# Head norms of a dilated attention computed inside the input projection instead of in the attention's own block

## The chip, the cores and the metric

The kernel runs on one core of a Trainium2 chip, in one launch. The metric is the device time of that core in microseconds (us). All weights (626 MB) are streamed from HBM, each once; everything is float32, and the large products are made of three products of split operands.

## What is computed

Two transformer blocks follow each other on 256 tokens of width 2048. The first block has an adaptive norm, an input projection `w_in` into u, q, k and v (1024 columns each), a state-space mixer on u, a dilated attention on q, k, v, an output projection and a gated FFN. The second block has two FFNs and another mixer. What the change touches is the attention of the first block:

```python
q = _rms(q.reshape(B, S, N_HEADS, HEAD_DIM), q_norm_w) * (HEAD_DIM ** -0.5)
k = _rms(k.reshape(B, S, N_HEADS, HEAD_DIM), k_norm_w)
slopes = exp2(-arange(1, 9))            # 8 heads of 128
bias = -slopes[:, None, None, None] * (dilation * dist)
scores = where(valid, q @ k.T + bias, MASK_VALUE)
```

`_rms` divides every head's vector of a token by the root of its mean square. So there are 16 head sums for each token (8 of q, 8 of k), 16 factors 1/root, and each score is q.k times a factor of the query and a factor of the key, plus a bias that depends on the distance and the head.

## The kernel before, in words

Activations lie transposed: features on the 128 partitions, tokens along the free axis (272 columns, of which 256 are the sequence). TensorE (PE), ScalarE (ACT), VectorE (DVE), GpSimd (POOL) and the DMA issuer SyncE (SP) have programs of their own, which meet in semaphores. The program is written in blocks; at the end of a block all engines meet.

**The input projection** (`products(pe, "w_in", ...)`, lines 551 to 553) is 32 chunks, counted by `m` from 0 to 31. A chunk of weights is a DMA of 1 MB into `raw`; ACT rounds it into `w_hi` (`split_hi`, L413), DVE subtracts into `w_lo` (`split_lo`, L418), and PE does 48 matmuls of 256 columns on it. Both `w_hi` and `w_lo` have two buffers, so ACT may split chunk m once chunk m-2 is multiplied. Between its splits DVE also accumulates rows of the adaptive weights for gate 1 (`condition`, L432, four products a chunk), and PE sums those over the partitions with `gather` (L437, four matmuls with one moving column of ones, for each of eight groups).

Beside each chunk a piece of the state-space mixer runs (`ssm_pe`, `ssm_act`, `ssm_dve`). It has 8 blocks `i`, and a block has three slots, `m = 5 + 3i + slot` on PE: slot 0 is 8 transposes (L1226), slot 1 the inputs to the states and the powers (L1236, L1246, L1247), slot 2 the outputs (L1261, L1263) and, before the change, the gathers of gate 1 (`GATE1_AT`). ACT and DVE do their part one chunk later.

**The attention's block** comes next. `heads_act`, `heads_pe` and `heads_dve` make the norms: ACT squares a head (L1437, 16 of them), PE sums it over the partitions with a one-hot matrix into 8 rows of PSUM (L1449), then DVE and ACT turn the two sets of 8x256 sums into factors (L1458 to L1465, the root on ACT at L1440). Only then does `v_pe` transpose v (L1511; the copies are ACT's, `v_act`, L1520). The values are copied after the two Gelu operations of the state-space output (L1680). `spread_pe` (L1477) spreads a head's factors over the partitions with a matmul, once for q and once for k, and `normed_dve` (L1489) multiplies both into `proj`. Then 16 units follow, two for each head: scores (L1538), bias (L1636), maximum (L1639, L1640), Exp (ACT, L1599), multiplicities and sum (L1653), division (L1655, L1656), transposes of the weights (L1550), product with v (L1561), and copies (L1606, L1615, L1665). Each engine runs through the units in a fixed, software-pipelined order (`units_pe`, `units_act`, `units_dve`); `spread_pe` and `normed_dve` for the next head stand in every second unit. GpSimd rearranges the state-space output meanwhile (`ynat`, L1690), as soon as the Gelus are done. SP loads `sel` and the bias table `dil` at the beginning of the block; the first weights of the next projection (`glu`) were loaded before.

## Time and profile before

| What | Value |
|---|---|
| median of 3 runs (lowest, highest) | 3295.01 us (3294.69, 3299.39) |
| the profiled execution | 3296.94 us, its span 3295.2 us |
| granted TensorE clock, mean | 0.968 |
| busy: PE, DVE, ACT, POOL | 95%, 58%, 37%, 6% |
| input projection's chunks on PE | about 136 to 400 us |
| attention's block | 401.4 to about 472.6 us |
| HBM over the span | 191 GB/s |

The span runs from the first to the last instruction. A busy share says how long an engine had an instruction; what a stage costs is seen from what ends its last wait. The granted clock is 1.0 where TensorE runs at 2.4 GHz and 0.5 where it runs at 1.2 GHz.

### The profile page before, as it was taken

The page shows a single profiled execution, that of the slowest core. Times are in us where ns is not written, and L with a number is a line of the kernel's source. Part 1 is how long each engine was busy: PE and PEld are TensorE (multiplying, and loading weights), DVE is VectorE, ACT ScalarE, POOL GpSimd, SP SyncE. Part 2 cuts the span into 40 slices and gives each one's busy share as a digit, 9 for nine tenths or more (in the row PEclk, how much of TensorE's full clock was granted, in tenths as well). Part 3 has the DMA queues.
Part 4 walks back from the last instruction along what each step waited for, and adds up shares of the span by engine and source line. Part 5 has one row for each costly group of instructions (what it writes and reads, how often), then busy time and mean ns, then how long its engine had stood idle before and what let it go on. Part 6 is the DMA issues. An engine that isn't in the chain of part 4 may idle for free.

```text
span 3295.2 us, 57562 instructions
## 1 busy us (share of the span) xinstructions
PE 3128.5 (95%) x25288; PEld 3075.6 (93%) x25288; DVE 1925.8 (58%) x1836; ACT 1209.4 (37%) x1061; POOL 203.9 (6%) x195
## 2 busy tenths in 40 slices
PE   3399978899999999999999999999999999999999
PEld 2399858899999999999999999999999999999999
DVE  7999769776444444745445544565556555454454
ACT  2264433333333333433333333344334333333333
POOL 3444130000000000000000000000030000000000
PEclk6699969999999999999999999999999999999999
DMA  9776608677555555555555555567635555555553
GB/s 337 255 258 243 234 34 289 225 262 276 177 182 190 183 188 188 183 173 172 178 175 170 179 176 170 178 185 141 128 127 183 186 180 191 181 189 184 187 186 133
DMA packets 328706, 630.52 MB, mean 191 GB/s; under 512 B 22452, under 2 KB 24008, under 8 KB 328280
## 3 DMA queue, kind: packets, MB, share of 16 engines
q1 hardware_dynamic: 317512, 624.79, 58.5%
q10 hardware_dynamic: 11040, 3.51, 0.5%
q8 instruction: 118, 1.93, 0.2%
q14 instruction: 36, 0.29, 0.0%
HBM read 626.16 MB, written 2.10 MB: 191 GB/s over the span
## 4 chain that ended last, share of the span: by engine, by line
PE 81%; DVE 3%; issue 1%; ACT 1%; DVEq 0%; ACTq 0%
PE ps L551 24%; PE ps L552 23%; PE ps L553 23%; PE ps L1859 2%; PE ps L1861 2%; PE ps L1860 2%; PE ps L1896 1%; PE ps L1898 1%; PE ps L1897 1%; DVE w_lo L418 1%; DVE accb L432 0%; ACT w_hi L413 0%; PE ps L1799 0%; PE ps L1790 0%; PE ps L1836 0%
## 5 line engine op out<-in xcount | busy, mean ns | idle before, releaser
L418 DVE TENSOR_TENSOR w_lo<-raw,w_hi 128x2048 fp32r<-128x2048 f32 x496 | 1141.9, 2303 | 1224.6 <-ACT w_hi L413 1224.5
L413 ACT ACTIVATE w_hi<-raw 128x2048 fp32r<-128x2048 f32 x496 | 949.7, 1915 | 1772.0 <-PE ps L553 1554.0
L551 PE MATMUL ps<-act_hi,w_hi 128*128 128x256 f32 (+1 forms) x4288 | 1223.1, 285 | 38.9 <-DVE w_lo L418 20.7
L552 PE MATMUL ps<-act_lo,w_hi 128*128 128x256 f32 (+1 forms) x4288 | 1220.8, 285 | 0.0
L553 PE MATMUL ps<-act_hi,w_lo 128*128 128x256 f32 (+1 forms) x4288 | 1218.8, 284 | 0.0
L551 PEld LDWEIGHTS ps<-act_hi,w_hi 128*128 128x128 f32 x4288 | 814.8, 190 | 42.2 <-issue 22.8
L551 PE MATMUL ps<-hid_hi,w_hi 128*128 128x256 f32 (+1 forms) x2880 | 815.6, 283 | 7.1 <-DVE w_lo L418 7.1
L553 PEld LDWEIGHTS ps<-act_hi,w_lo 128*128 128x128 f32 x4288 | 814.4, 190 | 0.0
L552 PEld LDWEIGHTS ps<-act_lo,w_hi 128*128 128x128 f32 x4288 | 814.2, 190 | 0.0
L553 PE MATMUL ps<-hid_hi,w_lo 128*128 128x256 f32 (+1 forms) x2880 | 813.9, 283 | 0.0
L552 PE MATMUL ps<-hid_lo,w_hi 128*128 128x256 f32 (+1 forms) x2816 | 796.2, 283 | 0.0
L551 PEld LDWEIGHTS ps<-hid_hi,w_hi 128*128 128x128 f32 x2880 | 544.3, 189 | 8.5 <-issue 7.3
L553 PEld LDWEIGHTS ps<-hid_hi,w_lo 128*128 128x128 f32 x2880 | 544.1, 189 | 0.0
L552 PEld LDWEIGHTS ps<-hid_lo,w_hi 128*128 128x128 f32 x2816 | 531.0, 189 | 0.0
L1859 PE MATMUL ps<-act_hi,w_hi 128*128 128x272 f32 x512 | 150.3, 294 | 0.0
L1861 PE MATMUL ps<-act_hi,w_lo 128*128 128x272 f32 x512 | 148.0, 289 | 0.0
L1860 PE MATMUL ps<-act_lo,w_hi 128*128 128x272 f32 x512 | 147.6, 288 | 0.0
L432 DVE SCALAR_TENSOR_TENSOR accg<-raw,cond,accg 128x512 f32<-128x512 f32 (+1 forms) x180 | 142.4, 791 | 5.3
L2042 POOL TENSOR_SCALAR sel_r<-sel 8x1024 fp32r<-8x1024 f32 x1 | 2.8, 2765 | 1753.3 <-DMA pw<-in_pool_w 1753.3
L1859 PEld LDWEIGHTS ps<-act_hi,w_hi 128*128 128x128 f32 x512 | 96.5, 188 | 3.3 <-issue 1.2
L432 DVE SCALAR_TENSOR_TENSOR acc<-raw,cond,acc 128x512 f32 (+1 forms) x120 | 95.3, 794 | 4.7
L1860 PEld LDWEIGHTS ps<-act_lo,w_hi 128*128 128x128 f32 x512 | 96.6, 189 | 0.0
(340 smaller groups left out, 2058.9 us busy)
## 6 DMA issues: line engine op xcount, KB each, us to landing
raw<-in_w_ada SPq DMA_DIRECT2D x96, 1024.0 KB, 5.3
raw<-in_ffn_w_gate SPq DMA_DIRECT2D x88, 1024.0 KB, 5.2
raw<-in_ffn_w_up SPq DMA_DIRECT2D x88, 1024.0 KB, 5.2
raw<-in_ffn_w_down SPq DMA_DIRECT2D x88, 1024.0 KB, 5.1
raw<-in_w_in SPq DMA_DIRECT2D x64, 1024.0 KB, 6.4
raw<-in_w_ffn_gate SPq DMA_DIRECT2D x44, 1024.0 KB, 5.2
raw<-in_w_ffn_up SPq DMA_DIRECT2D x44, 1024.0 KB, 5.2
raw<-in_w_ffn_down SPq DMA_DIRECT2D x44, 1024.0 KB, 5.1
```

The lines of the kernel that those rows point to most:

```text
L413: act.activation(w_hi[b][:, :, :], raw[j % RING][:, :, :], ACT.Copy).then_inc(hi_ready, 1)
L418: dve.tensor_tensor(w_lo[b][:, :, :], raw[j % RING][:, :, :], w_hi[b][:, :, :].bitcast(F32), ALU.subtract).then_inc(lo_ready, 1)
L432: dve.scalar_tensor_tensor(out=acc, in0=w, scalar=x, in1=acc, op0=ALU.mult, op1=ALU.add).then_inc(acc_step, 1)
L551: pe.matmul(o, whi, hi[:, k, cols], start=(k == 0 and not (shared and m % 2)), stop=False)
L552: pe.matmul(o, whi, lo[:, k, cols], start=False, stop=False)
L553: mm = pe.matmul(o, wlo, hi[:, k, cols], start=False, stop=(k == CK * p.cpg - 1 and not (shared and m % 2 == 0)))
L1859: pe.matmul(ps[:, o, 0:T], whi, act_hi[:, k, :], start=(k == 0), stop=False)
L1860: pe.matmul(ps[:, o, 0:T], whi, act_lo[:, k, :], start=False, stop=False)
L1861: mm = pe.matmul(ps[:, o, 0:T], wlo, act_hi[:, k, :], start=False, stop=(k == KT - 1))
L1896: pe.matmul(out_at(g, o), whi, hi, start=(first and t == 0 and o % 2 == 0), stop=False)
L1897: pe.matmul(out_at(g, o), whi, lo, start=False, stop=False)
L1898: mm = pe.matmul(out_at(g, o), wlo, hi, start=False, stop=(last and t == CK - 1 and o % 2 == 1))
```

## The change

Squares: ACT squares four heads at once beside chunks 14, 18, 22 and 25, into the place of v in `proj` that is not yet written. Sums: PE sums each set with 8 matmuls of one moving column (`heads_pe`), beside chunks 17, 20, 23 and 26, so that the sums of 128 tokens lie on the partitions; all 32 columns of sums (16 heads, two halves of the tokens) go to PSUM bank 7 next to the gate's sums. These and the gathers of gate 1 now stand in slot 0 (`small_sums`), with new places for the gathers. ACT copies the sums beside chunk 29; DVE adds the epsilon beside chunk 30, ACT takes the root beside chunk 31, behind that chunk's weight split, and DVE finishes the factors in five operations on 128x32 after the last chunk's work (`heads_dve`, `m == 32`).

In the attention's block the query's factor is no longer multiplied into q. It is the per-partition scalar of the operation that adds the bias; so the slope is now multiplied into the table on the host, and `dil` holds all 8 heads (128x3072 instead of 128x384, next to `mult`, 128x384, in four transfers instead of two). The key's factors are transposed back into 8 rows (`factors_pe`, `factors_act`), and the spread and `normed_dve` are for k alone, with both gains in one column. The first two groups of v are copied by DVE.

```diff
-        "dilated": np.concatenate(dist + mult, axis=1), "causal": np.concatenate(mask, axis=1),
+        "dilated": np.concatenate([np.float32(s) * d for s in slopes for d in dist], axis=1), "mult": np.concatenate(mult, axis=1), "causal": np.concatenate(mask, axis=1),
...
+        hs = at("hs", [P, 5, 32])
...
-        dil = at("dil", [P, 768], offset=pw_at)
+        dil = at("dil", [P, HEADS, 384], offset=pw_at)
+        mult = at("mult", [P, 384], offset=pw_at + 4 * 384 * HEADS)
...
             k = it * 4 * p.groups + 4 * g
+            if k == 24:
+                act.wait_ge(hs_mm, 4)
             if k == 28:
                 act.wait_ge(mod_sum, 16)
             act.activation(proj[:, k:k + 4, cols], src, ACT.Copy).then_inc(bank_free[g % 2], 1)
...
+        def small_sums(pe, m, i):
+
+            if i >= 2:
+                pe.wait_ge(y_ready, i - 1)
+            if m in GATE1_AT:
+                g = GATE1_AT.index(m)
+                pe.wait_ge(acc_step, CK * (byname["w_in"].before["V"] + 4 * g + 4))
+                gather(pe, accg1[:, g % 2, :], 7, SEQ + 4 * g)
+            if m in HEADS_AT:
+                heads_pe(pe, m)
+
         def ssm_pe(pe, m):
             i, slot = ssm_turn(m, 0)
+            if slot == 0 and i == BLOCKS:
+                small_sums(pe, m, i)
             if slot == 0 and i < BLOCKS:
 
                 b = i % 2
+                small_sums(pe, m, i)
...
-                if m in GATE1_AT:
-                    g = GATE1_AT.index(m)
-                    pe.wait_ge(acc_step, CK * (byname["w_in"].before["V"] + 4 * g + 4))
-                    gather(pe, accg1[:, g % 2, :], 7, SEQ + 4 * g)
...
-        GATE1_AT = (7, 10, 13, 16, 22, 25, 28)
+        HEADS_AT = (17, 20, 23, 26)
+
+        def heads_act(act, m):
+            n = {14: 0, 18: 1, 22: 2, 25: 3}.get(m)
+            if n is not None:
+                act.wait_ge(bank_free[n % 2], group_index(byname["w_in"], (n + 2) // 2, n % 2) + 1)
+                if n:
+                    act.wait_ge(hs_mm, n)
+                act.activation(proj[:, 24:28, SEQ_COLS], proj[:, 8 + 4 * n:12 + 4 * n, SEQ_COLS], ACT.Square).then_inc(hs_sq, 1)
+            if m == 31:
+                act.wait_ge(hs_ms, 1)
+                act.activation(hs[:, 2, :], hs[:, 1, :], ACT.Sqrt).then_inc(hs_root, 1)
+
+        def sums_act(act, m):
+            if m == 29:
+                act.wait_ge(hs_mm, 4)
+                act.wait_ge(y_mm, BLOCKS - 1)
+                act.activation(hs[:, 0, :], ps[:, 7, SEQ + 32:SEQ + 64], ACT.Copy).then_inc(hs_read, 1)
+
+        def heads_pe(pe, m):
+            n = HEADS_AT.index(m)
+            pe.wait_ge(hs_sq, n + 1)
+            for e in range(4):
+                for s_ in range(2):
+                    c = SEQ + 32 + 16 * (n // 2) + 8 * s_ + 4 * (n % 2) + e
+                    mm = pe.matmul(ps[:, 7, c:c + 1], proj[:, 24 + e, META + P * s_:META + P * s_ + P], ones[:, 0:1],
+                                   start=True, stop=True, skip_group_check=True)
+            mm.then_inc(hs_mm, 1)
+
+        def heads_dve(dve, m):
+            if m == 30:
+                dve.wait_ge(hs_read, 1)
+                dve.tensor_scalar(hs[:, 1, :], hs[:, 0, :], 1.0 / P, EPS, ALU.mult, ALU.add).then_inc(hs_ms, 1)
+            if m == 32:
+                dve.wait_ge(hs_root, 1)
+                link(dve, "dve", dve.reciprocal(hs[:, 2, :], hs[:, 2, :]))
+                link(dve, "dve", dve.tensor_tensor(hs[:, 3, :], hs[:, 2, :], hs[:, 2, :], ALU.mult))
+                link(dve, "dve", dve.tensor_tensor(hs[:, 3, :], hs[:, 3, :], hs[:, 1, :], ALU.mult))
+                link(dve, "dve", dve.tensor_scalar(hs[:, 3, :], hs[:, 3, :], -0.5, 1.5, ALU.mult, ALU.add))
+                dve.tensor_tensor(hs[:, 4, :], hs[:, 2, :], hs[:, 3, :], ALU.mult).then_inc(hs_rstd, 1)
+
+        GATE1_AT = (5, 8, 14, 17, 20, 26, 29)
...
-                                  beside=lambda m: ssm_act(act, m))
+                                  beside=lambda m: (sums_act(act, m), ssm_act(act, m), heads_act(act, m)))
...
-                dve.tensor_scalar(qk_gain[:, 0:1], vecs[:, V_QK:V_QK + 1], scale, None, ALU.mult)
-                dve.tensor_copy(qk_gain[:, 1:2], vecs[:, V_QK + 1:V_QK + 2])
+                dve.scalar_tensor_tensor(out=qk_gain[:, 1:2], in0=vecs[:, V_QK:V_QK + 1], scalar=scale, in1=vecs[:, V_QK + 1:V_QK + 2],
+                                         op0=ALU.mult, op1=ALU.mult)
...
-                          peel=4, beside=lambda m: ssm_dve(dve, m))
+                          peel=4, beside=lambda m: (ssm_dve(dve, m), heads_dve(dve, m)))
                 ssm_dve(dve, 32)
+                heads_dve(dve, 32)
...
+        def spread_pe(pe, h):
+
+            if h:
+                pe.wait_ge(hs_done, h)
+            pe.matmul(ps[:, 4, 0:SEQ], sel[:, h, :], rq[:, 4, 0:SEQ], start=True, stop=True).then_inc(hs_bc, 1)
+
+        def normed_dve(dve, h):
+
+            dve.wait_ge(hs_bc, h + 1)
+            x = proj[:, 16 + h, SEQ_COLS]
+            dve.scalar_tensor_tensor(out=x, in0=x, scalar=qk_gain[:, 1:2], in1=ps[:, 4, 0:SEQ], op0=ALU.mult, op1=ALU.mult).then_inc(hs_done, 1)
+
+        def factors_pe(pe):
+
+            pe.wait_ge(hs_rstd, 1)
+            for s_ in range(2):
+                mm = pe.transpose(ps[0:HEADS, 5, P * s_:P * s_ + P], hs[:, 4, 16 + 8 * s_:24 + 8 * s_], ident)
+            mm.then_inc(kf_t, 1)
+
+        def factors_act(act):
+            act.wait_ge(kf_t, 1)
+            act.activation(rq[:, 4, 0:SEQ], ps[0:HEADS, 5, 0:SEQ], ACT.Copy).then_inc(kf_copied, 1)
...
+
+        def v_pe(pe, groups):
+            for g in groups:
+                kt, h0 = g // 2, 4 * (g % 2)
                 if g >= 2:
-                    pe.wait_ge(v_copied, g - 1)
...
+        def v_copy(g):
+
+            kt, h0 = g // 2, 4 * (g % 2)
+            return vt[:, kt, h0:h0 + 4, :], ps[:, 6 + g % 2, :].rearrange("p (h n) -> p h n", h=4)
+
+        def v_act(act):
+            for g in (2, 3):
+                act.activation(*v_copy(g), ACT.Copy).then_inc(v_copied, 1)
+
+        def v_dve(dve):
+            for g in (0, 1):
+                dve.wait_ge(v_t, g + 1)
+                dve.tensor_copy(*v_copy(g)).then_inc(v_half, 1)
+
...
+                        dve.wait_ge(bias_in, 16)
+                    dve.scalar_tensor_tensor(out=x, in0=ps[:, u, 0:n], scalar=hs[:, 4, 8 * qt + h:8 * qt + h + 1], in1=dil[:, h, P * qt:P * qt + n],
+                                             op0=ALU.mult, op1=ALU.add).then_inc(logit, 1)
...
         with block:
             @block.sync
             def _(sp):
-                sp.dma_start(sel[:, :, :], a["sel"].rearrange("a (h p) -> a h p", h=HEADS)).then_inc(mix_in, 16)
-                sp.dma_start(dil[:, :], a["dilated"]).then_inc(mix_in, 16)
+                sp.dma_start(sel[:, :, :], a["sel"].rearrange("a (h p) -> a h p", h=HEADS)).then_inc(sel_in, 16)
+                bias = a["dilated"].rearrange("p (h n) -> p h n", h=HEADS)
+                sp.dma_start(dil[:, 0:2, :], bias[:, 0:2, :]).then_inc(mix_in, 16)
+                sp.dma_start(mult[:, :], a["mult"]).then_inc(mix_in, 16)
+                sp.dma_start(dil[:, 2:HEADS, :], bias[:, 2:HEADS, :]).then_inc(bias_in, 16)
 
             @block.scalar
             def _(act):
-                heads_act(act, 0, "s")
-                heads_act(act, 0, "r")
+                factors_act(act)
                 for h in range(2):
                     act.activation(proj[:, 4 * h:4 * h + 4, SEQ_COLS], proj[:, 4 * h:4 * h + 4, SEQ_COLS],
                                    ACT.Gelu_apprx_tanh).then_inc(gelu_done, 1)
-                v_act(act, 0)
-                units_act(act, 0)
+                v_act(act)
+                units_act(act)
 
             @block.gpsimd
             def _(pool):
@@ -1692,18 +1656,19 @@
 
             @block.vector
             def _(dve):
-                heads_dve(dve, 0)
+                v_dve(dve)
                 dve.wait_ge(mix_in, SSM_IN + 32)
-                units_dve(dve, 0)
+                units_dve(dve)
 
             @block.tensor
             def _(pe):
-                heads_pe(pe, 0)
-                pe.wait_ge(mix_in, SSM_IN + 32)
-                pe.wait_ge(hs_ms, 2)
-                v_pe(pe, 0)
-
-                units_pe(pe, 0, nothing)
+                factors_pe(pe)
+                v_pe(pe, (0, 1))
+                pe.wait_ge(sel_in, 16)
+                pe.wait_ge(kf_copied, 1)
+                spread_pe(pe, 0)
+                v_pe(pe, (2, 3))
+                units_pe(pe)
 
 
```

The order in which PE works through the middle of the projection, before chunk 17, then the same place after the change. The lines of the chunk's matmuls are L551 to L553 before and L555 to L557 after; `eb` is the operand of the state-space transposes, `accg` that of the gathers, and `proj` that of the head sums.

```order
L551 MATMUL ps<-act_hi,w_hi_54 128x256
L552 MATMUL ps<-act_lo,w_hi_54 128x256
L553 MATMUL ps<-act_hi,w_lo_56 128x256
L1226 MATMUL ps<-const,eb 128x128 x8
L551 MATMUL ps<-act_hi,w_hi_53 128x256
```

```order
L555 MATMUL ps<-act_hi,w_hi_54 128x256
L556 MATMUL ps<-act_lo,w_hi_54 128x256
L557 MATMUL ps<-act_hi,w_lo_56 128x256
L441 MATMUL ps<-const,accg_83 128x1 x4
L1307 MATMUL ps<-const,proj 128x1 x8
L1246 MATMUL ps<-const,eb 128x128 x8
L555 MATMUL ps<-act_hi,w_hi_53 128x256
```

Twelve matmuls of one column now stand between two chunks, ahead of the eight transposes.

PE from the end of the projection into the attention's block, before and after (`accg` is the last gather of gate 1, then the branches to the next block):

```order
L437 MATMUL ps<-const,accg_82 128x1 x4
L1270 UNCONDITIONAL_BRANCH
L1699 UNCONDITIONAL_BRANCH
L1449 MATMUL ps<-sq,const 8x256 x16
L1511 MATMUL ps<-const,proj 128x128 x16
L1477 MATMUL ps<-rq,sel 128x256 x2
L1538 MATMUL ps<-proj 128x128
```

```order
L441 MATMUL ps<-const,accg_83 128x1 x4
L1327 UNCONDITIONAL_BRANCH
L1663 UNCONDITIONAL_BRANCH
L1495 MATMUL ps<-const,hs 8x128 x2
L1509 MATMUL ps<-const,proj 128x128 x8
L1483 MATMUL ps<-rq,sel 128x256
L1509 MATMUL ps<-const,proj 128x128 x8
L1537 MATMUL ps<-proj 128x128
```

The 16 one-hot sums are gone, two transposes take their place, and the first spread stands in the middle of v's transposes.

DVE in the same place, before and after:

```order
L432 SCALAR_TENSOR_TENSOR accg_82<-raw_52,cond,accg_82 128x512 x4
L1375 TENSOR_TENSOR mod<-ps,bada 128x32
L1270 UNCONDITIONAL_BRANCH
L1693 UNCONDITIONAL_BRANCH
L1458 TENSOR_SCALAR rq<-ps 8x256
L1460 RECIPROCAL rq<-rq 8x256
L1462 TENSOR_TENSOR rq<-rq 8x256
L1463 TENSOR_TENSOR rq<-rq 8x256
L1464 TENSOR_SCALAR rq<-rq 8x256
L1465 TENSOR_TENSOR rq<-rq 8x256
```

```order
L436 SCALAR_TENSOR_TENSOR accg_83<-raw_52,cond,accg_83 128x512 x4
L1317 RECIPROCAL hs<-hs 128x32
L1318 TENSOR_TENSOR hs<-hs 128x32
L1319 TENSOR_TENSOR hs<-hs 128x32
L1320 TENSOR_SCALAR hs<-hs 128x32
L1321 TENSOR_TENSOR hs<-hs 128x32
L1433 TENSOR_TENSOR mod<-ps,bada 128x32
L1327 UNCONDITIONAL_BRANCH
L1657 UNCONDITIONAL_BRANCH
L1525 COPY vt<-ps 128x512 x2
L1489 SCALAR_TENSOR_TENSOR proj<-proj,qk_gain,ps 128x256
L1605 SCALAR_TENSOR_TENSOR lg<-ps,hs,dil 128x128
```

The chain of the factors (shown before for the first of its two sets, q and k) moved ahead of the block's end, on 32 columns instead of 256, and DVE begins the block with copies of v.

## Rows read from the trace of the kernel before

**Rows 1.** Windows: us, busy time and instructions of each engine, granted clock, DMA share, GB/s.
```profile
300.00:400.00 100.00, 99.96 (x877) 99.07 (x876) 92.69 (x126) 43.80 (x72) 20.18 (x20) 1.00 0.74 263
...
448.00:468.00 20.00, 19.16 (x58) 13.52 (x58) 16.04 (x66) 6.55 (x22) 3.96 (x2) 0.56 0.00 1
```

**Rows 2.** Timeline, block's beginning: start, length, engine, line, operation, [idle before <- releaser].
```profile
401.49 0.72 ACT L1437 ACTIVATE sq<-proj 128x256 f32<-128x256 f32 x2 [0.28 <-PEq L1270]
...
417.43 2.00 ACT L1680 ACTIVATE proj<-proj 128x1024 f32<-128x1024 f32 x2
419.34 1.06 ACT L1520 ACTIVATE vt<-ps 128x512 f32<-128x512 f32 x2
...
422.59 1.28 ACT L1599 ACT_TABLE_LOAD   x1
...
424.08 0.87 DVE L1489 SCALAR_TENSOR_TENSOR proj<-proj,qk_gain,ps 128x256 f32<-128x256 f32 x2 [4.53 <-PE ps L1477]
```

**Rows 3.** Timeline of the units: DVE's L1653 begins a unit's second half.
```profile
429.97 0.44 DVE L1653 SCALAR_TENSOR_TENSOR ex<-ex,dil 128x128 f32<-128x128 f32 x1
...
458.67 0.29 DVE L1653 SCALAR_TENSOR_TENSOR ex<-ex,dil 128x128 f32<-128x128 f32 x1
...
472.31 0.29 DVE L1665 TENSOR_TENSOR act_lo<-ps,act_hi 128x128 fp32r<-128x128 f32 x1 [1.27 <-ACT act_hi L1606]
...
454.41 2.07 PE L1477 MATMUL ps<-rq,sel 8*128 8x256 f32 x4
```

**Rows 4.** Timeline of PE in the projection: slots of three state-space blocks.
```profile
202.73 3.64 PE L1236 MATMUL ps<-proj,bt 128*128 128x64 f32 x16 [2.30 <-ACT bt L1128]
...
215.75 0.95 PE L437 MATMUL ps<-const,accg 128*128 128x1 f32 x8
...
256.94 1.90 PE L1236 MATMUL ps<-proj,bt 128*128 128x64 f32 x16
...
266.64 0.95 PE L437 MATMUL ps<-const,accg 128*128 128x1 f32 x8
```

**Rows 5.** Timeline at chunk 26: DVE's split, then PE's first matmul on it.
```profile
350.13 2.29 DVE L418 TENSOR_TENSOR w_lo<-raw,w_hi 128x2048 fp32r<-128x2048 f32 x1
...
352.56 0.35 PE L551 MATMUL ps<-act_hi,w_hi 128*128 128x256 f32 x1
```

**Rows 6.** Timeline of PE: the two longest runs of one-column matmuls.
```profile
598.16 2.74 PE L437 MATMUL ps<-const,accb 128*128 128x1 f32 x24
...
601.52 0.39 PE L551 MATMUL ps<-act_hi,w_hi 128*128 128x256 f32 x1 [0.63 <-DVE w_lo L418]
...
830.48 3.63 PE L437 MATMUL ps<-const,accg 128*128 128x1 f32 x32
```

**Rows 7.** Windows behind runs and gaps; the granted clock is the third number from the end.
```profile
206.00:208.00 2.00, 2.00 (x12) 1.63 (x12) 1.96 (x3) 0.01 (x1) 0.00 (x0) 0.50 0.91 347
...
602.00:604.00 2.00, 2.00 (x13) 2.00 (x12) 1.89 (x4) 0.00 (x0) 0.00 (x0) 0.54 0.46 150
...
689.50:692.00 2.50, 1.14 (x10) 0.94 (x9) 2.04 (x1) 1.72 (x1) 0.00 (x0) 1.00 0.56 107
...
835.00:836.00 1.00, 1.00 (x7) 1.00 (x7) 1.00 (x1) 0.00 (x0) 0.00 (x0) 0.50 0.00 0
```

**Rows 8.** Timeline of SP, and DMA traffic of 400 to 410 us in 40 slices.
```profile
401.83 0.35 SPq L1673 DMA_DIRECT2D dil<-in_dilated  x1
...
GB/s 0 0 0 0 0 0 0 0 0 0 131 156 172 221 332 455 234 37 0 0 0 0 0 66 0 0 0 0 0 0 0 0 0 0 0 0 0 0 0 0
```

**Rows 9.** Timeline of POOL's copies, and DVE's scaling beside them and after them.
```profile
419.52 32.52 POOL L1690 TENSOR_SCALAR ynat<-proj 32x512 f32<-32x512 f32 x16 [72.86 <-ACT proj L1680]
...
438.94 0.95 DVE L1656 TENSOR_SCALAR pn<-ex,st 128x256 f32<-128x256 f32 x1
...
455.07 0.35 DVE L1656 TENSOR_SCALAR pn<-ex,st 128x256 f32<-128x256 f32 x1
```

**Rows 10.** DVE at the end of the projection: its last wait before the block's end.
```profile
400.12 0.19 DVE L1375 TENSOR_TENSOR mod<-ps,bada 128x32 f32<-128x32 f32 x1 [5.49 <-PE ps L437]
```

256 lines of the change are left out of this document (70 added, 186 removed).

## The prediction

> **What bounds the kernel now.** I read the windows first. From 300 to 400 us PE is busy for 99.96 of 100 us at the full clock [rows 1], so the input projection is bound by PE, and whatever is added to PE there costs its full time. DVE is close behind: it is busy for 92.69 us, and at chunk 26 its split ends at 352.42 (350.13 + 2.29) and PE takes it up at 352.56 [rows 5]. It has to be asked whether DVE would decide there instead; it gets nothing of weight from the change, so more work on PE only gives it more lead.
>
> The second view is the timeline of the attention's block. It begins at 401.49, and the first unit reaches its second half on DVE (L1653) at 429.97 [rows 2, 3]. Those 28.5 us are a chain through four engines: squares and sums, two sets of factors, Gelu and v's copies, spread and the first products. The third view is the units: from 429.97 to 458.67 are five pairs, 5.74 us each, and the last copy of the block begins at 472.31 [rows 3]. From 448 to 468 PE is busy for 19.16 of 20 us, with a mean clock of 0.56 [rows 1]: it is PE at 1.2 GHz that sets the pace. DVE is second with 16.04 us. Behind the block everything follows in the same order as before, so I let it move as a whole.
>
> **The change part by part.** *Head sums on PE.* They are 4 x 8 matmuls of one column; the trace shows such a float32 matmul as two instructions (a gather of four is x8, rows 4), so 64. The longest run of them is 32 in 3.63 us, 0.113 us each [rows 6]. 64 x 0.113 = **+7.2 us**, all on the bound engine.
>
> *The moved gathers.* There are as many as before, at the same price. One comes free: PE waits 2.30 us at 202.73 for ACT's copy `bt` (slot 1 of block 1, chunk 9), since ACT was busy with the strided copies of u [rows 4]. The gather of group 1 was at chunk 10 and now stands at chunk 8, ahead of that wait, so it eats into it: **-0.9 us** (0.95 in rows 4), and the gap shrinks to 1.4 us. Before, the clock was at 0.50 behind that gap [rows 7], and from the slot's beginning to the next gather PE took 215.75 - 202.73 = 13.0 us, against 266.64 - 256.94 = 9.7 us for the same work later: the low clock cost 3.3 us [rows 4]. A gap of about 1.4 us elsewhere (2.50 less 1.14 busy, at 689.5) left the clock at 1.00 [rows 7]. So I expect it to stay up: **-3.3 us**, with 0 as the other end.
>
> *The clock behind the new runs.* At chunks 17, 20 and 26 sums and gather make 24 one-column instructions in a row. Eight never lowered the clock in the projection (1.00 from 300 to 400, rows 1). 24, followed by 0.6 us of idling, did: 0.54 in 602 to 604; and 32 did without any idling: 0.50 at 835 [rows 6, 7]. The new runs are like the shorter of those without its gap, with transposes behind them. A fall costs between 0 and the 3.3 us of the one measured above; one of half that size in three places: **+1.7 us**.
>
> [...]
>
> *Everything else in the projection* I cost at nothing. Four squares of 1024 elements on ACT, some 1.0 us each (as a Gelu, half of 2.00 in rows 2), beside 56% idle time; their waits for `hs_mm` are for sums one chunk old. If that cover were gone, DVE's next split would be late, and PE with it. The root, with its table load (1.28, as in rows 2), stands behind chunk 31's split, and DVE's five small operations behind its last accumulation, where DVE waits 5.49 us for the last gather [rows 10]; beyond that they would delay the end of the block. The gathers' wait for `acc_step` is never for later work than the split that PE has to await anyhow. Sum of the projection: 7.2 - 0.9 - 3.3 + 1.7 = **+4.7 us**, from 3.0 to 11.4.
>
> *The beginning of the attention's block.* Gone are 16 squares and sums and both sets of factors. ACT's path is now: wait for the two transposes and copy the factors, some 0.9 us; table load 1.28; Gelus 2.00; two copies of v 1.06; table load 1.28 [rows 2]. From 401.5 that gives the first Exp at 408.0. DVE's path is: two copies of v, the tables' landing, the product for head 0, scores, bias. The old transfers of 0.43 MB, of which the larger is issued at 401.83, had landed by 404.5 [rows 8]; `sel`, the first two heads' table and `mult` are 0.62 MB, so I take 405. Behind PE's wait for `sel` stand v's transposes of groups 2 and 3, and ACT's copies wait for those; they have time until the Gelus end at 405.7. Head 0's product is 0.44 (half of L1489's 0.87, rows 2), then scores and bias, the same for the second unit, about 4 us in all from 405: L1653 begins at 409.0 instead of 429.97. With PE at its lower clock, which its idleness here makes likely, 0.5 us later: **-20.5 us**, from -19 (tables at 406.5) to -21.5.
>
> *The units.* Each of the seven spreads within the units loses its half for q: 1.03 us on PE at the low clock (half of 2.07, rows 3), 0.43 on DVE. What of it shows lies between the two, since with a lighter PE, DVE is late next: 0.7 for each of six pairs, **-4.2 us** (-2.6 to -6.2). Against it stands POOL. Its copies last 32.5 us from the Gelus' end, and beside them DVE's scaling takes 0.95 instead of 0.35 us [rows 9]. Before, they covered four pairs (to 452.0); now, from 405.7 to 438.2, they cover six. Two more pairs with two such operations each: up to 2.4, of which I take **+1.0 us**. The bias through a column of factors replaces an operation of the same shape. The bias table's remainder of 1.2 MB has until the fifth unit, some 8 us, and 455 GB/s was seen at the peak [rows 8].
>
> [...]
>
> *Sum:* 4.7 - 20.5 - 4.2 + 1.0 = **-19.0 us**. The profiled execution took 3296.9 us, so 3277.9; it was 1.9 above the median of the runs, so I forecast **3276 us**. A measurement of this kernel tells some 0.2%, 6.6 us, from no change.
>
> **The rivals.** *The clock falls at all three runs, and behind chunk 9 as before.* For it: 24 of these instructions with a short gap did it. Against it: dense work is on both sides. The projection gives 7.2 - 0.9 + 3 x 1.7 = 11.4, the sum is -12.3: 3282.7. Chance 0.17.
>
> *The clock never falls and PE is the whole pace of the units:* 3.0 - 21.5 - 6.2 = -24.7, 3270.3. For it: PE's 96% in the units. Against: DVE's load beside POOL. Chance 0.18.
>
> *The transfers decide the beginning:* if the four share the engines evenly, all 1.8 MB must land before the first product, 3 us later than I take: 3279. Against it: one queue, in order of issue. Chance 0.06.
>
> *The factors aren't ready when the block begins,* so that their chain is only moved: if the root comes behind more of ACT's work than I see, the block's end moves by up to the chain's length, five small operations and a root, some 3 us: 3279. Against: the 5.49 us of waiting [rows 10]. Chance 0.04.
>
> *Slower than before:* the runs don't only lower the clock, they keep it low through the chunks behind them, since every third chunk begins with another one. From 215.75 to 266.64 are six chunks with their slots, 8.5 us each [rows 4]; at half clock each would take up to 8.5 us more. The forecast's 19.0 us are used up after two to three such chunks; six of the twelve from 17 to 28 would give 3276 + 51 = 3327. Against it: at 602 and 835 dense matmuls followed at once, as here, and by the mean of 0.968 such stretches are rare. Chance 0.02.
>
> **How the numbers follow.** My forecast has 0.53, with 3271 to 3281 for its own range. The first rival lies above and the second below, together 0.35, so both are taken in with the ends of the units' terms: **3267 to 3287**. Faster by over 0.2% means below 3288.4: 0.94; within 0.2%: 0.04; slower: 0.02.
>
> **What would show it.** After the change PE should show runs of one-column matmuls of 1.8 us at four places, and the projection end 3 to 6 us later; a wait for `bt` of 1.4 us at chunk 9, with a clock of 1.0 behind it; the clock between 276 and 365 tells the rivals apart. The successor of L1653 should first begin some 8 us after the block's start instead of 28.5, pairs should take 5.0 us, and from the end of the units on all should be as before. I am wrong if the block's first product waits for a DMA beyond 407, if DVE idles in the projection's end for the root, or if the pairs still take 5.7 us.

## The result, and the profile after the change

The changed kernel takes 3278.2 us, median of 4 runs (3276.54 to 3283.66), against 3295.75 us (3294.69 to 3299.39, 4 runs) for the kernel before on the same chip: a ratio of 0.9946, with a 95% interval from 0.9934 to 0.9958. The forecast was 3276.0 us with a range from 3267 to 3287. The profiled execution took 3276.54 us (span 3274.6), 20.4 less than the profiled one of before; the medians differ by 17.5. The mean granted clock is 0.971.

The traces give TensorE's clock as a share of its full speed; no run gives a frequency. At a granted clock of 0.50 the 256-column matmuls of a chunk begin 0.213 us apart (14 of them from 301.17 to 303.94 us in g_slot2), at 1.00 they begin 0.118 us apart (17 of them from 387.93 to 389.82 us in b_r32). By an estimate from the first number, with one column taken a tick, 256 columns in 0.213 us are 1.2 GHz, and full speed is twice that; the second number, 2.2 columns a ns, lies a little below. Where the forecast and the expectations say 1.2 GHz, the traces show 0.50.

Here and below the projection's stretch runs from chunk 5's state-space transposes to the last gather of gate 1. Where a gather stands in slot 0, one of 0.8 us lies ahead of that stretch, which in the kernel before lies inside it.

| Stretch | before | after | difference |
|---|---|---|---|
| start to chunk 5's slot | 172.9 | 171.1 | -1.8 |
| chunk 5's slot to the last gather | 226.24 | 231.19 (230.38 without its gather) | +4.95 |
| last gather to the first L1653 / L1618 | 30.83 | 11.48 | -19.35 |
| from there to the last L1665 / L1627 | 42.34 | 38.51 | -3.83 |
| from there to the end of the span | 2822.9 | 2822.3 | -0.6 |

The change adds nothing of weight to the first row or to the last one: I take these 2.4 us of the 20.6 in the spans as scatter between executions. In the other kernels made from the changed one the first row lies between 170.5 and 173.6 us. What remains is 18.2.

The windows of the changed kernel that answer to [rows 1] (us, then busy time and instructions of PE, PEld, DVE, ACT and POOL, granted clock, DMA share, GB/s):

```profile
300.00:400.00 100.00, 100.00 (x870) 99.50 (x870) 92.06 (x127) 45.30 (x76) 19.62 (x20) 0.98 0.74 257
424.00:444.00 20.00, 17.22 (x60) 11.81 (x60) 18.14 (x68) 7.55 (x24) 16.98 (x9) 0.67 0.00 1
```

PE still has no idle time between 300 and 400 us. In the units the order has turned round in this execution: DVE is busy for 18.14 of 20 us, PE for 17.22, where in [rows 1] PE had 19.16. (In an execution of b_early, whose units are the same, the clock stayed at 0.50, and PE is first again; that window is shown further down.)

PE's timeline in the projection of the changed kernel (start, length, engine, line, operation, idle time before and its releaser):

```profile
191.93 1.05 PE L441 MATMUL ps<-const,accg 128*128 128x1 f32 x8 [0.22 <-DVE accg L436]
192.84 1.07 PE L1246 MATMUL ps<-const,eb 128*128 128x128 f32 x8
194.22 0.35 PE L555 MATMUL ps<-act_hi,w_hi 128*128 128x256 f32 x1 [0.31 <-DVE w_lo L422]
...
200.90 2.00 PE L1256 MATMUL ps<-proj,bt 128*128 128x64 f32 x16 [0.81 <-ACT bt L1134]
...
270.92 1.93 PE L1307 MATMUL ps<-const,proj 128*128 128x1 f32 x16
...
353.33 1.48 PE L1246 MATMUL ps<-const,eb 128*128 128x128 f32 x8
...
402.29 0.95 PE L441 MATMUL ps<-const,accg 128*128 128x1 f32 x8
```

A set of head sums is 16 instructions in 1.93 us. The wait for `bt` at chunk 9 has shrunk from 2.30 us [rows 4] to 0.81, because PE had already waited twice for DVE just before. Behind it the work that took 3.64 us takes 2.00, and the clock stayed up (1.00 from 200.9 to 203.0 us).

The beginning of the attention's block in the changed kernel (the same columns), to be laid beside [rows 2]:

```profile
404.67 0.38 PE L1495 MATMUL ps<-const,hs 128*8 128x128 f32 x2 [1.43 <-PEq L1327]
...
404.89 1.76 PE L1509 MATMUL ps<-const,proj 128*128 128x128 f32 x8
...
406.57 1.22 PE L1483 MATMUL ps<-rq,sel 8*128 8x256 f32 x2
406.77 2.00 ACT L1644 ACTIVATE proj<-proj 128x1024 f32<-128x1024 f32 x2
...
407.72 1.97 PE L1509 MATMUL ps<-const,proj 128*128 128x128 f32 x8
...
409.06 0.48 DVE L1489 SCALAR_TENSOR_TENSOR proj<-proj,qk_gain,ps 128x256 f32<-128x256 f32 x1 [1.68 <-DMA mult<-in_mult]
...
409.59 0.50 PEld L1537 LDWEIGHTS ps<-proj 128*128 128x128 f32 x2 [0.30 <-DVE proj L1489]
409.59 0.79 PE L1537 MATMUL ps<-proj 128*128 128x128 f32 x2
...
411.64 0.40 ACT L1581 ACTIVATE ex<-lg,st 128x128 f32<-128x128 f32 x1
412.73 0.48 DVE L1605 SCALAR_TENSOR_TENSOR lg<-ps,hs,dil 128x256 f32<-128x256 f32 x1 [0.67 <-PE ps L1537]
...
413.77 0.28 DVE L1618 SCALAR_TENSOR_TENSOR ex<-ex,mult 128x128 f32<-128x128 f32 x1
```

The first product (L1489) waits 1.68 us for the tables, and L1618 begins 9.15 us after the block's start at 404.62 (its first DMA issue), where the forecast had some 8. It looks as if the tables cost the difference. Look at PE as well: v's second half of transposes ends at 409.7, just when the first scores start, and the weight load of these scores had waited only 0.30 us for the product. So without the tables' lateness the scores could have come at most 0.3 us sooner.

### The profile page after: what moved, and what is told of

Its sections match the earlier page's. It is cut to its first block, busy times and chain, and to the rows that moved or that the text cites. A ratio compares the mean times of both kernels' runs of the same rounds, so it can differ in the third digit from the quotient of the medians.

```text
span 3274.6 us, 57581 instructions
## 1 busy us (share of the span) xinstructions
PE 3119.8 (95%) x25306; PEld 3075.3 (94%) x25306; DVE 1916.5 (59%) x1823; ACT 1206.7 (37%) x1048; POOL 201.5 (6%) x195
## 3 DMA queue, kind: packets, MB, share of 16 engines
q8 instruction: 118, 1.93, 0.2%
## 4 chain that ended last, share of the span: by engine, by line
PE 82%; DVE 3%; issue 1%; ACT 1%; DVEq 0%; ACTq 0%
PE ps L555 24%; PE ps L556 24%; PE ps L557 24%; PE ps L1824 2%; PE ps L1826 2%; PE ps L1825 2%; PE ps L1861 1%; PE ps L1863 1%; PE ps L1862 1%; DVE w_lo L422 1%; DVE accb L436 0%; ACT w_hi L417 0%; PE ps L1764 0%; PE ps L1755 0%; PE ps L1801 0%
## 5 line engine op out<-in xcount | busy, mean ns | idle before, releaser
L555 PE MATMUL ps<-act_hi,w_hi 128*128 128x256 f32 (+1 forms) x4288 | 1221.8, 285 | 40.3 <-DVE w_lo L422 22.2
L557 PE MATMUL ps<-act_hi,w_lo 128*128 128x256 f32 (+1 forms) x4288 | 1217.5, 284 | 0.0
L555 PEld LDWEIGHTS ps<-act_hi,w_hi 128*128 128x128 f32 x4288 | 814.5, 190 | 43.6 <-issue 24.3
L555 PE MATMUL ps<-hid_hi,w_hi 128*128 128x256 f32 (+1 forms) x2880 | 814.7, 283 | 7.1 <-DVE w_lo L422 7.1
L557 PEld LDWEIGHTS ps<-act_hi,w_lo 128*128 128x128 f32 x4288 | 813.5, 190 | 0.0
L557 PE MATMUL ps<-hid_hi,w_lo 128*128 128x256 f32 (+1 forms) x2880 | 813.0, 282 | 0.0
L555 PEld LDWEIGHTS ps<-hid_hi,w_hi 128*128 128x128 f32 x2880 | 544.1, 189 | 8.5 <-issue 7.3
L557 PEld LDWEIGHTS ps<-hid_hi,w_lo 128*128 128x128 f32 x2880 | 543.6, 189 | 0.0
```

The costliest lines, as they stand in the source:

```text
L555: pe.matmul(o, whi, hi[:, k, cols], start=(k == 0 and not (shared and m % 2)), stop=False)
L557: mm = pe.matmul(o, wlo, hi[:, k, cols], start=False, stop=(k == CK * p.cpg - 1 and not (shared and m % 2 == 0)))
```

## The experiments

Twelve kernels ran. All are made from the changed kernel, except g_before_gathers.

| Kernel | median, us | ratio to before (95%) | projection's stretch | gather to first L1618 | units | clock fell behind chunks |
|---|---|---|---|---|---|---|
| before | 3295.75 | | 226.24 | 30.83 | 42.34 | 9 |
| changed | 3278.2 | 0.9946 (0.9934 to 0.9958) | 230.38 | 11.48 | 38.51 | 26 |
| g_before_gathers | 3296.24 | 1.0000 (0.9991 to 1.0009) | 224.56 | 32.02 | 42.36 | none |
| g_slot2 | 3289.58 | 0.9976 (0.9967 to 0.9986) | 243.85 | 11.45 | 37.74 | 9, 16, 19, 22, 25, 28 |
| g_sums_one | 3275.87 | 0.9933 (0.9919 to 0.9947) | 225.17 | 11.79 | 38.31 | 9 |
| g_sums_twice | 3293.54 | 0.9989 (0.9980 to 0.9998) | 242.66 | 11.52 | 39.86 | 9, 17, 20, 26 |
| u_two_spreads | 3287.02 | 0.9968 (0.9955 to 0.9982) | 231.29 | 13.24 | 42.30 | 17, 26 |
| u_pool_later | 3308.78, one run | | 231.13 | 11.18 | 38.67 | 17, 26 |
| b_early | 3277.87 | 0.9943 (0.9929 to 0.9956) | 231.32 | 11.52 | 39.82 | 17, 26 |
| b_early_order | 3277.79 | 0.9939 (0.9926 to 0.9953) | 231.22 | 9.82 | 38.80 | 17, 26 |
| b_spread_r | 3275.98 | 0.9940 (0.9926 to 0.9953) | 231.20 | 9.06 | 38.36 | 17, 26 |
| b_r32 | 3270.14 | 0.9923 (0.9909 to 0.9936) | 227.30 | 11.37 | 39.35 | 9 |
| b_best | 3270.09 | 0.9919 (0.9906 to 0.9933) | 227.31 | 9.40 | 38.65 | 9 |
| u_both | 3306.19, one run | | 231.20 | 8.95 | 34.24 | 17, 26 |

The stretches are each from one profiled execution. The last column is read from its windows of 1 us: behind each chunk named the granted clock was 0.50 in at least two of them (in b_early from 272 to 274 and from 354 to 356 us), and 0.97 or more everywhere else in the stretch but at the two ends of such a fall. In the two kernels with one run GpSimd's copies come late and the next projection waits for them, so their totals say nothing: PE's longest wait behind the units, for DVE's split, was 36.5 us in u_pool_later and 36.4 in u_both.

Medians of different rows were taken on different chips, each beside its own kernel before. By the ratios some differences against the changed kernel come out otherwise than by the medians: g_slot2 9.9 us instead of 11.4, g_sums_one -4.3 instead of -2.3, g_sums_twice 14.2 instead of 15.3, u_two_spreads 7.3 instead of 8.8 (the differences of the ratios times 3296 us).

### The gathers alone, in the kernel before (g_before_gathers)

```diff
+        def small_sums(pe, m, i):
+
+            if i >= 2:
+                pe.wait_ge(y_ready, i - 1)
+            if m in GATE1_AT:
...
             if slot == 0 and i < BLOCKS:
...
+                small_sums(pe, m, i)
...
             if slot == 2:
...
-                if m in GATE1_AT:
...
-        GATE1_AT = (7, 10, 13, 16, 22, 25, 28)
+        GATE1_AT = (5, 8, 14, 17, 20, 26, 29)
```

> The kernel before with one part of the change alone: the gathers of gate 1 stand in slot 0 at chunks 5, 8, 14, 17, 20, 26, 29 instead of slot 2. Theory (a gather ahead of the wait for bt at chunk 9 shortens it from 2.30 to about 0.8-1.4 us and the clock stays up behind it): the stretch from chunk 5's transposes to the last gather falls from 226.2 to 222.0 us, the total by 4.2, to about 3291.5. Rival (the clock's fall there has nothing to do with the length of the gap): only the gap's 0.9 to 1.5 us, total about 3294.8, and the clock is 0.5 behind the gap as before. Second rival (gathers in slot 0 now wait for DVE's accumulation, since they come two chunks' slots earlier): new waits on accg, total not below 3295.

No change in the total: the total is that of the second rival. The wait for `bt` was 1.55 us, so 0.75 gained, and the clock did stay up behind it (1.00 from 202 to 206 us). But PE's waits in the rest of the projection (engine and line, what it waited for, us in total, times, longest), which the kernel before does not have, took it back:

```profile
PE ps L551 <- DVE w_lo L418: 2.3, 4, 1.4
PE ps L437 <- DVE accg L432: 0.3, 1, 0.3
```

Two of the mechanisms are there, and the size isn't: PE gained 0.75 and about 3.2 and ran into DVE, which gave back 2.6: 2.3 by its splits and 0.3 by an accumulation. DVE is busy for 92.69 of 100 us [rows 1], which leaves PE little to gain on it. The waits are mostly for the splits, not for the accumulation that the second rival named. The stretch, with its gather of 0.8 added, is 225.4 against 226.2.

### Sums and gathers in slot 2 (g_slot2)

```diff
-            if slot == 0 and i == BLOCKS:
-                small_sums(pe, m, i)
             if slot == 0 and i < BLOCKS:
...
-                small_sums(pe, m, i)
...
             if slot == 2:
...
+                small_sums(pe, m, i)
...
-        HEADS_AT = (17, 20, 23, 26)
+        HEADS_AT = (16, 19, 22, 25)
...
-        GATE1_AT = (5, 8, 14, 17, 20, 26, 29)
+        GATE1_AT = (7, 10, 13, 16, 22, 25, 28)
```

> The changed kernel with the gathers back in slot 2 at their old places and the head sums beside them in slot 2 (chunks 16, 19, 22, 25), nothing else altered. Theory (what the slot is worth is the wait for bt at chunk 9 and the clock behind it): that wait is 2.3 us again with the clock at 0.5 behind it, so +4.2 us against the changed kernel, about 3282.4 and 235.4 us from chunk 5 to the last gather; the clock falls behind no more than one of the three runs of 24. Rival (slot 2 is where PE waits for y_ready and h_ready, so the sums fill time that was idle): about 3278 or less. Rival (runs of 24 in front of 64-column matmuls lower the clock each time): three falls, 3287.

The last rival comes nearest, and my theory covers only a part. As it said, the wait at chunk 9 is 2.31 us again, with the clock at 0.50 behind it. But the stretch is 13.5 us longer where 4 to 5 were expected, and the clock falls behind every one of the four sets of sums, behind the set of 16 instructions without a gather (chunk 19) as behind those of 24. The window there:

```profile
300.00:304.00 4.00, 4.00 (x20) 4.00 (x21) 3.96 (x7) 2.16 (x10) 2.10 (x1) 0.50 0.93 303
```

PE is busy without a break and still at 0.50. The clock was at 0.50 from 272 to 274 us, 299 to 305, 330 to 336, 361 to 363 and 388 to 390. It fell behind chunk 28 too, where only a gather stands; behind the gathers at chunks 7, 10 and 13 of the same kernel, and behind all of them in the kernel before, it did not. In slot 2 the sums are followed by the state-space outputs, 128x64 and 128x63; in slot 0 by eight transposes of 128x128. That is one difference between the places that the rows show; whether it is the one that counts was not tried alone. So the choice of the slot is worth 11.4 us by the medians (3289.58 - 3278.2), more than the head sums' whole price; some 4 us of it belong to chunk 9.

### One eighth of the sums (g_sums_one), and twice the sums (g_sums_twice)

```diff
-            for e in range(4):
-                for s_ in range(2):
-                    c = SEQ + 32 + 16 * (n // 2) + 8 * s_ + 4 * (n % 2) + e
-                    mm = pe.matmul(ps[:, 7, c:c + 1], proj[:, 24 + e, META + P * s_:META + P * s_ + P], ones[:, 0:1],
+            for s_ in range(1):
+                c = SEQ + 32 + 8 * n
+                mm = pe.matmul(ps[:, 7, c:c + 8], proj[:, 24, META + P * s_:META + P * s_ + P], ones[:, 0:8],
```

```diff
-            for e in range(4):
+            for e in (0, 1, 2, 3) * 2:
```

> The changed kernel with one 8-column matmul in place of each set's eight 1-column matmuls: seven eighths of the head sums are left out, so q and k are scaled by wrong factors; all waits and squares stay. Theory (PE bounds the projection and 64 one-column instructions cost 0.113 us each): 56 instructions fewer, -6.3 us, and the fall of the clock behind chunk 26 goes with the run of 24, -1.6 more: about 3270.3, 223.3 us from chunk 5 to the last gather. Rival (DVE's splits have become the bound in places, as the small new waits for w_lo of 1.0 us in sum suggest): at most 4 us come back and the waits for w_lo stay or grow. Rival (the clock's falls aren't the runs' doing): -6.3 alone, 3271.9, a fall between 330 and 365 us remains.

> The changed kernel with every head sum made twice (the second overwrites the first, the output is unchanged): runs of 40, 40, 32 and 40 one-column instructions at chunks 17, 20, 23, 26. Theory (64 more instructions at 0.113 us, and runs as long as this lower the clock as the run of 32 at 830 us did, 1.6 us each, where one fell before): +7.2 + 3 x 1.6 = +12.0, about 3290. Rival (the clock doesn't care for such runs between dense chunks): +7.2, 3285.4. Rival (half clock stays for several chunks once runs are this long): over 3295.

The first diff is that of g_sums_one, the second that of g_sums_twice. With 56 instructions fewer the stretch is 225.17. It has one fall, behind chunk 9, of 3.2 us (from chunk 8's transposes to chunk 11's 29.79 us against 26.62 in b_early, with the same wait of 1.55); b_early has two falls of about 1.6 (from chunk 17's transposes to chunk 20's 28.79 against 27.18 in the changed kernel, which had no fall there). The falls cancel, and 231.32 - 225.17 = 6.15 us is the price of 56 instructions in these two executions, against 6.3 expected. PE waited for DVE's splits for only 0.35 us here, but this execution had lost 3.2 us at chunk 9, which gives DVE a lead; in g_before_gathers, without that fall and without sums, it was 2.3 us for the splits and 2.6 for DVE in all. So the rival of DVE as the bound is not excluded for the executions in which the clock stays up at chunk 9. The total came down by only 2.3 us, less than either of the first two forecasts here; that this is DVE's share is not shown.

With the sums doubled the stretch is 17.5 us longer than with one eighth, for 120 instructions (13.6 at 0.113) and three falls, behind chunks 17, 20 and 26. Behind chunk 23, where 32 instructions stand without a gather, none: no window of 1 us from 313 to 367 us is under 0.97. The median is 15.3 above the changed kernel's; expected were 12. The fall behind chunk 9, which the changed kernel's profile lacks, may be the rest; no run shows it.

That fall can go either way. The wait at chunk 9 is 1.55 to 1.58 us in eleven of the profiled kernels, and PE's instructions up to it are the same. In four of them (g_sums_one, g_sums_twice, b_r32, b_best) the clock fell behind it and in seven not. The first two differ from the changed kernel only behind that place, so their edit isn't what decides. What does decide stays open, as each kernel was profiled once. Two windows of the same place, first of b_early, then of g_sums_one:

```profile
204.00:208.00 4.00, 4.00 (x36) 3.96 (x34) 3.93 (x4) 2.01 (x5) 3.30 (x3) 1.00 0.77 249
```

```profile
204.00:208.00 4.00, 4.00 (x23) 3.60 (x23) 3.86 (x7) 2.25 (x5) 0.00 (x0) 0.50 1.02 369
```

36 instructions against 23 in the same 4 us.

### Transfers before the block begins (b_early)

```diff
                 stream(sp, "w_in")
+                sp.wait_ge(y_mm, BLOCKS)
+                sp.dma_start(sel[:, :, :], a["sel"].rearrange("a (h p) -> a h p", h=HEADS)).then_inc(sel_in, 16)
...
                 stream(sp, "glu", rest=False)
```

The other three transfers follow `sel` there in the order of the block.

> The changed kernel with the four transfers of sel and the tables issued before the block begins, behind PE's last state-space matmul (397 us), where their place is free. Theory (the first product waits 1.3 us for the tables, but behind it PE still runs through v's transposes until 409.7, so the first scores come when they came): L1489 begins at about 3.2 us after the block's start instead of 4.4, and the first L1618 at most 0.3 us sooner; total within 1 us of 3278. Rival (the landing of the tables is what holds the beginning, the forecast's error of 1.1 us): the first L1618 at about 8.0 us after the start instead of 9.15, total 1.2 lower.

The theory holds. The product (L1489 in the changed kernel, L1495 here) no longer waits for a DMA, and the first L1618 comes 11.52 us behind the last gather, as before 11.48. From the timeline of b_early:

```profile
408.38 1.97 PE L1515 MATMUL ps<-const,proj 128*128 128x128 f32 x8
408.55 0.48 DVE L1495 SCALAR_TENSOR_TENSOR proj<-proj,qk_gain,ps 128x256 f32<-128x256 f32 x1 [0.53 <-PE ps L1489]
...
410.14 0.63 PE L1543 MATMUL ps<-proj 128*128 128x128 f32 x2
```

The product is done at 409.03 and the scores start at 410.14: eight transposes of v stand in front of them on PE, at a granted clock of 0.50 (408.4 to 410.1 us). These had themselves waited 0.65 us for DVE's copy of v's first group.

### The beginning in another order (b_early_order)

```diff
                     scores(s_ + 1)
+                if s_ == 0:
+                    v_pe(pe, (2, 3))
...
                     act.activation(ex[:, u, 0:n], lg[:, u, 0:n], ACT.Exp, bias=st[:, u, 1:2]).then_inc(expd, 1)
+                    if s_ == 0:
+                        v_act(act)
...
             normed_dve(dve, 0)
+            v_dve(dve)
...
-                v_pe(pe, (0, 1))
+                v_pe(pe, (0,))
...
                 spread_pe(pe, 0)
-                v_pe(pe, (2, 3))
+                v_pe(pe, (1,))
```

> As the early transfers, and the beginning in another order: PE spreads head 0 behind one group of v's transposes and does the last two groups behind the second unit's scores; DVE multiplies head 0 before it copies v; ACT copies its two groups of v behind the first Exp. Theory (PE's 3.7 us of transposes at 1.2 GHz and ACT's chain up to the first Exp, at 7.0 us after the block's start, hold the beginning together): first Exp at 5.5, first L1618 at 6.4 to 7.0 us after the start instead of 9.15, so about -2.5 us, 3275.7, the units as long as before. Rival (it is only moved: the last groups of v now hold the first product with v): first L1618 earlier, but the units longer by the same.

The successor of L1618 (L1629 here) comes 1.7 us sooner, 9.82 us behind the last gather, and the units keep their length:

```profile
408.34 0.63 PE L1543 MATMUL ps<-proj 128*128 128x128 f32 x2
...
411.06 1.92 PE L1515 MATMUL ps<-const,proj 128*128 128x128 f32 x8
...
412.35 0.28 DVE L1629 SCALAR_TENSOR_TENSOR ex<-ex,mult 128x128 f32<-128x128 f32 x1
```

The scores now start at 408.34, ahead of the last eight transposes. So the order of the beginning, with PE's transposes in front, and not the tables, was what held it. The edit moves work on PE, DVE and ACT at once; what each of them gave was not tried. The expected 2.5 us was too much, and the median moved by 0.4 us, which can't be told from nothing.

### What sets the pace of the units (u_two_spreads, u_pool_later, b_spread_r, u_both)

```diff
-            pe.matmul(ps[:, 4, 0:SEQ], sel[:, h, :], rq[:, 4, 0:SEQ], start=True, stop=True).then_inc(hs_bc, 1)
+            for w in range(2):
+                mm = pe.matmul(ps[:, 4, SEQ * w:SEQ * w + SEQ], sel[:, h, :], rq[:, 4, 0:SEQ], start=True, stop=True)
...
-            x = proj[:, 16 + h, SEQ_COLS]
+            for w in range(2):
+                x = proj[:, 8 + 8 * w + h, SEQ_COLS]
```

```diff
                 pool.wait_ge(gelu_done, 2)
+                pool.wait_ge(p_norm, 16)
```

```diff
-            pe.matmul(ps[:, 4, 0:SEQ], sel[:, h, :], rq[:, 4, 0:SEQ], start=True, stop=True).then_inc(hs_bc, 1)
+            pe.matmul(ps[:, 4, 0:SEQ], sel_r[:, h, :], rq_r[:, 3, 0:SEQ], start=True, stop=False)
+            pe.matmul(ps[:, 4, 0:SEQ], sel_r[:, h, :], rq_r[:, 4, 0:SEQ], start=False, stop=True).then_inc(hs_bc, 1)
```

> The changed kernel with the second spread and the second product of every head put back (PE spreads the key's factors twice, DVE multiplies the second copy and the gain into q too; q is then scaled twice, so the scores differ). Theory (the halved spread is what made a pair of units shorter): a pair of units takes 5.7 us again instead of 5.1, the units 38.5 + 4.2 = 42.7 us from the first to the last copy, the beginning 0.5 to 1.0 later, the total about +5 (2.6 to 6.2). Rival (GpSimd's copies beside DVE set the pace, the spread lies in PE's idle time): less than +2 in the units.

> The changed kernel with GpSimd's 16 copies held back until the last unit's weights are divided, so that no unit has them beside it; the gated projection behind then begins up to 32 us later and the total says nothing. Read the units alone, 38.5 us now. Theory (PE at 1.2 GHz sets the pace, and GpSimd costs a pair that it covers only 0.5 us, as the sum of the forecast had it): 35 to 36 us. Rival (each scaling beside GpSimd takes 0.95 instead of 0.35 us and all of it is on the path: 2 x 0.6 for each of six pairs): 31.3 us. Rival (nothing of it is on the path): 38.5 us.

> As the early transfers with the new order (b_early_order), and the spread is made of two products of fp32r operands (the key's factors split into a high and a low part, sel rounded by GpSimd beforehand) instead of one of float32. Theory (the units are paced by PE at 1.2 GHz: held-back GpSimd changed nothing and a second spread cost 0.6 a pair): a spread of float32 takes 0.85 to 1.22 us there, two of fp32r about 0.43, so a pair gets 0.4 to 0.8 us shorter, the units 38.8 - 4 = 35 us, total about 3274. Rival (DVE is the pace as soon as PE is lighter; a pair of DVE's operations takes about 4.7): 37 us, 3276. Rival (PE only waits longer, the clock falls the same): no change.

> The fp32r spreads (b_spread_r) and GpSimd's copies held back until the units are done, together. Each alone left the units at 38.4 and 38.7 us, against 38.5 in the changed kernel. Theory (two bounds of nearly the same size: PE at 1.2 GHz, 99% busy where GpSimd is silent, and DVE beside GpSimd, 94% busy where PE is lighter; taking one away uncovers the other): with both gone the units fall to what DVE needs without GpSimd, 83% of 5.06, or 4.2 to 4.5 us a pair, 33 to 35 us from the first to the last copy. Rival (neither engine is the pace, the units are a chain of waits through PE, DVE and ACT): 38 us again. The total says nothing, as the gated projection behind waits for GpSimd.

The diffs are those of u_two_spreads, u_pool_later and b_spread_r; u_both has the last two. b_spread_r and u_both also have the early transfers and the new order of b_early_order. The second spread brings the units back to 42.30 us (+3.8): that part of the change has the size of its term. The beginning goes to 13.24 (+1.8, where 0.5 to 1.0 was expected), and the total rises by 8.8 us, more than the 2.6 to 6.2 expected; what makes up the rest is open. Holding GpSimd back leaves the units at 38.67 against 38.51, where the theory wanted 35 to 36. A lighter spread leaves them at 38.36, where it wanted 35. Both together give 34.24, as expected. The same window, 420 to 440 us, of u_pool_later and then of u_both:

```profile
420.00:440.00 20.00, 19.81 (x61) 14.15 (x60) 16.60 (x68) 7.25 (x25) 0.00 (x0) 0.50 0.00 1
```

```profile
420.00:440.00 20.00, 17.02 (x70) 12.10 (x68) 18.72 (x80) 9.32 (x28) 0.00 (x0) 0.78 0.00 1
```

Without GpSimd PE is the bound, 19.81 of 20 us at 0.50, a pair of units in 5.06 us. With a lighter PE and GpSimd beside it, DVE is, as the same window of b_spread_r shows:

```profile
420.00:440.00 20.00, 16.60 (x58) 12.06 (x58) 18.84 (x68) 8.16 (x24) 19.38 (x11) 0.64 0.00 1
```

At a clock of 0.50 the lighter spread, two products of fp32r, holds PE for 0.72 us (428.84 to 429.56 us in b_spread_r, where 0.43 was expected), that of float32 for 1.15 us (421.55 to 422.70 us in u_pool_later). With both gone a pair takes 4.3 us, DVE is at 18.72 and PE's clock rises to 0.78. Two bounds of nearly one size stood behind each other, and taking away either showed only the other.

One thing has to be kept apart from this: the clock in the units differs between executions of the same code. In b_early, whose units are those of the changed kernel, it stayed at 0.50 through all of them, as it did in u_pool_later but for some 3 us near their end. Its window:

```profile
420.00:440.00 20.00, 19.86 (x60) 14.06 (x59) 17.64 (x66) 7.20 (x25) 19.40 (x10) 0.50 0.00 1
```

Its units took 39.82 us, and those of g_sums_twice, also at 0.50 throughout, 39.86. Against these two, which are nearest to u_pool_later in the clock, holding GpSimd back gave 1.2 us (38.67), not nothing.

How GpSimd lengthens DVE's work is seen in the groups of instructions of VectorE (line, operation, shape, count, busy time, mean ns), first the changed kernel, then u_pool_later:

```profile
L1621 DVE TENSOR_SCALAR pn<-ex,st 128x256 f32<-128x256 f32 x8 | 5.0, 627 | 0.3
...
L1621 DVE TENSOR_SCALAR pn<-ex,st 128x128 f32<-128x128 f32 x8 | 4.2, 526 | 0.3
```

```profile
L1621 DVE TENSOR_SCALAR pn<-ex,st 128x256 f32<-128x256 f32 x8 | 2.8, 354 | 0.3
L1621 DVE TENSOR_SCALAR pn<-ex,st 128x128 f32<-128x128 f32 x8 | 2.3, 286 | 0.3
```

The mean delay is 0.24 to 0.27 us, and the longest single one took 1.05 us instead of 0.29. GpSimd's copies take 2.04 us each (L1654, 16 in 32.62 us). No scaling in the changed kernel was delayed by more than 0.8 us: the delay is there, and it is shorter than a whole copy.

### Cheaper sums, and all together (b_r32, b_best)

```diff
-                act.activation(proj[:, 24:28, SEQ_COLS], proj[:, 8 + 4 * n:12 + 4 * n, SEQ_COLS], ACT.Square).then_inc(hs_sq, 1)
+                act.activation(proj_r[:, 24:28, SEQ_COLS], proj[:, 8 + 4 * n:12 + 4 * n, SEQ_COLS], ACT.Square).then_inc(hs_sq, 1)
...
-                    c = SEQ + 32 + 16 * (n // 2) + 8 * s_ + 4 * (n % 2) + e
-                    mm = pe.matmul(ps[:, 7, c:c + 1], proj[:, 24 + e, META + P * s_:META + P * s_ + P], ones[:, 0:1],
+                    c = SEQ + 32 + 2 * (16 * (n // 2) + 8 * s_ + 4 * (n % 2) + e)
+                    mm = pe.matmul(ps[:, 7, c:c + 2], proj_r[:, 24 + e, META + P * s_:META + P * s_ + P], ones_r[:, 0:2],
```

> The changed kernel with the head sums from squares rounded to fp32r, two columns each: a float32 one-column matmul is two instructions, so 32 instructions instead of 64. Theory (0.113 us each, but DVE's splits have little lead left: with no sums at all in the kernel before, gathers in slot 0 gave 2.6 us of waits for w_lo): -3.6 of PE's work, 1 us of it given back as waits for w_lo, and with runs of 16 instead of 24 the two falls of the clock behind chunks 17 and 26 (1.5 us each) go: -5, 226.5 us from chunk 5's transposes to the last gather instead of 231.3, total 3273. Rival (the falls are due to the place and stay): -3, 3275. Rival (a two-column fp32r matmul is as dear as two one-column instructions): no change.

> All of it together: early transfers, new order of the beginning, fp32r spreads, fp32r sums. If the parts add: against the changed kernel -1.65 (beginning), -4 (units), -5 (projection), so about 3267.5. If the shorter projection runs into DVE's splits and the units into DVE's operations: about 3272.

What the theory of b_r32 takes from runs stands at these places: 0.113 us an instruction in [rows 6]; the waits in g_before_gathers, where 2.3 us were for `w_lo` and 0.3 for `accg`, so the 2.6 are those for DVE in all; the two falls, 1.6 us each, in b_early (28.79 against 27.18 us for the first). That 16 instructions leave the clock up, b_early shows at chunk 23 only, in slot 0: 16 instructions in 1.84 us from 324.74, and a clock of 1.00 from 327 to 333. In g_slot2 it fell behind 16 too. The 1 us given back was an estimate.

From the timeline of b_r32 at chunk 17:

```profile
273.84 0.95 PE L442 MATMUL ps<-const,accg 128*128 128x1 f32 x8
274.65 1.03 PE L1308 MATMUL ps<-ones_r,proj_r 128*128 128x2 f32 x8
275.55 1.09 PE L1247 MATMUL ps<-const,eb 128*128 128x128 f32 x8
```

A set is now 8 instructions, in 1.03 us instead of 1.93, and no fall of the clock is left behind chunks 17 and 26 (1.00 from 276 to 282 and from 353 to 359 us): the stretch is 227.30, 4.0 less than in b_early, in an execution that had the fall of 3.2 us behind chunk 9. PE's only wait in it is that at chunk 9; DVE gave nothing back. The median is 3270.14, 8.1 us below the changed kernel, where 5 was expected. 32 instructions fewer at 0.110 and two falls of 1.6 make 6.7; the rest is not explained. b_best has the same median, between the two totals that were expected (3267.5 and 3272): its beginning is 2 us shorter than that of b_r32, and the rest is within the scatter of five runs (3266.53 to 3273.75). Its units stay at 38.65, as those of b_spread_r did while GpSimd ran beside them.

## Why the prediction was right, and where its steps were not

**The head sums, +7.2.** Right as time on PE: 56 instructions cost 6.15 us, 0.110 each. In the medians, leaving them out gave back only 2.3 us.

**The moved gathers, -0.9 and -3.3.** The mechanism was right and the certainty was not. In the kernel before ACT made 16 copies of u (L717, 195.48 to 201.64 us) ahead of `bt` (L1128, 1.02 us from 201.66), and `bt` is what PE waited for until 202.73. The wait shrank by 0.75 us (to 1.55; in the profiled execution to 0.81), and where the clock stayed up it was worth 3.2 us. But with a wait of 1.55 us it stayed up in seven executions and fell in four, so the term is between 0 and -3.3, as its bounds said. What the step left out is DVE: alone in the kernel before, the edit is worth nothing, since 2.6 us came back as waits for DVE. With the sums' work on PE beside it these waits are 0.2 us in b_early and 1.3 in the changed kernel. The terms do not stand on their own: the sums fill some of the time in which PE would have waited. The forecast had asked whether DVE would decide and answered that more work on PE only gives it more lead; the part of the change that takes time off PE was not asked about.

**The clock behind the new runs, +1.7.** Its size was off: in six of seven executions with this placement it fell behind chunks 17 and 26, about 1.6 us each, +3.2; in the one profiled first, only behind 26. Behind chunk 20, with the same 24 instructions, it fell in none of the seven. Its cause is not seen: PE had no idle time around these falls (busy for 9.00 of 9 us from 266 to 275 and for 11.00 of 11 from 346 to 357 in b_early). With the projection at +4.95 in the profiled execution and +5.9 in b_early (231.32 + 0.8 - 226.24), the sum of +4.7 was near.

**Everything else in the projection at nothing.** Right but for one small wait: a gather waited 0.22 us for DVE's accumulation (191.93 above), which the forecast had ruled out. DVE waited 7.82 us for the last gather at the end of the projection, more than in [rows 10], so neither the root nor the five small operations showed:

```profile
403.28 0.19 DVE L1433 TENSOR_TENSOR mod<-ps,bada 128x32 f32<-128x32 f32 x1 [7.82 <-PE ps L441]
```

**The beginning, -20.5.** It was -19.35. No run puts the old chain of squares, sums and factors back alone; that this term is its removal is read from the two timelines. The step that failed is the one that said v's transposes of groups 2 and 3 stand behind the spread and "have time until the Gelus end". They have, nearly, for ACT; but on PE they stand in front of the first scores, at a granted clock of 0.50 (407.7 to 409.7 us), and the scores came at 409.6. The lower clock that the step counted on is there, 0.61 from 404.6 to 406.6 us and 0.50 from there to 414; that idleness brings it is not shown. The tables landed later than 405 too (4.4 us after the block's start instead of 3.5). The two delays ran side by side and were of nearly one length, so taking away the tables' alone gave nothing (b_early).

**The units, -4.2 + 1.0.** They gave -3.8. The step on GpSimd is not settled: against the changed kernel, holding it back gave nothing; against executions with the clock at 0.50 throughout it gave 1.2 us for all the pairs that GpSimd covers. The +1.0 stood for two of six such pairs, so it was too much by either reading. The step on the spread, 0.7 a pair, gives -3.8 by u_two_spreads. That DVE is late next was said, and is what b_spread_r met.

**The rivals.** The rival with all falls (3282.7) was half true of the projection: two falls behind the runs, and none behind chunk 9 in the seven executions with this placement. The one with the units at PE's pace (3270.3) had the right bound for a silent GpSimd, but the clock did fall. The one for the other side did not happen: in the changed kernel the clock was back at 1.00 from 358 us on, 5 us after the sums of chunk 26. Nor did the factors come late, by DVE's wait of 7.82 us; and that the transfers decide the beginning is answered by b_early.

**Sum against result.** -19.0 was forecast for the execution. The stages gave -18.2 in the one profiled, and with the projection of b_early -17.3, close to the 17.5 of the medians, though one execution and a median need not agree so well. Against that stand 1.1 us too much in the beginning and 1.2 too little in the projection, and 0.6 on the other side in the units. The forecast is 2.2 us below the median. Some of that is luck: the -3.3 at chunk 9 came true in the profiled execution of the changed kernel, but not in four of the eleven with a wait of 1.55 us, and the runs of this kernel alone scatter by 7 us.

## What to carry to other kernels

Try small matmuls in more than one place, and count their price as instructions plus a possible fall of the clock: the same sums and gathers cost some 10 us more in slot 2, in front of 64-column matmuls, than in slot 0, in front of full transposes. That what follows them is the cause was not tried alone. Before counting on a saving on the bound engine, read how far the next engine is behind: here 2.6 of 4 us came back at once, and in the units two edits that changed the units by under 0.2 us each gave 4.3 us together. Compare the granted clock before two executions are compared: the same units took 37.7 to 39.9 us. In a short block with TensorE at a granted clock of 0.50, look at the order of its own transposes before blaming a transfer: here it was worth 1.7 us, and the transfers nothing.

## What the hardware showed that I had not expected

- The granted clock fell behind runs of 16 and 24 one-column instructions in front of 128x64 matmuls (four of four in g_slot2) and behind one of its four gathers of 8, and it fell behind runs of 24 in front of 128x128 transposes in two of three places, with PE busy throughout.
- The same instructions with the same wait of 1.55 us were followed by a clock of 1.0 in seven executions and 0.5 in four, a difference of 3.2 us in kernels whose runs scatter by 3 to 8.
- Two columns of fp32r cost one instruction where one column of float32 costs two: 8 in 1.03 us instead of 16 in 1.93.
- In the units PE was busy for 19.81 of 20 us at a granted clock of 0.50 (u_pool_later), and for 17.02 of 20 at a mean of 0.78 where its spreads were lighter (u_both).
